# Second-layer attention of a two-block transformer kernel: rounds in two parts, the last q, k unit ahead of the third v unit, low parts as steps of their own

## The reference, cut to what matters

```python
s1 = jnp.einsum('bhqd,bhkd->bhqk', qb1, k1).astype(jnp.float32) * scale
s2 = jnp.einsum('bhqd,bhkd->bhqk', qb2, k2).astype(jnp.float32) * scale
p1 = jax.nn.softmax(jnp.where(mask, s1, -jnp.inf), axis=-1)
p2 = jax.nn.softmax(jnp.where(mask, s2, -jnp.inf), axis=-1)
a = (p1 - lam * p2).astype(v.dtype)
return jnp.einsum('bhqk,bhkd->bhqd', a, v)
...
o = o * lax.rsqrt(jnp.mean(jnp.square(o), axis=-1, keepdims=True) + RMS_EPS)
o = (o * subln_g.astype(jnp.float32) * (1.0 - lambda_init)).astype(x.dtype)
return _merge_blocks(o) @ w_out
```

## Time and profile before

| | before |
|---|---|
| median of 3 runs | 2318.71 us (2317.28 to 2320.51) |
| the profiled execution's own time | 2320.3 us |
| its span | 2318.5 us |
| mean granted TensorE clock | 0.964 |
| PE, DVE, ACT, POOL busy | 94%, 50%, 43%, 41% of the span |
| the stage that the change touches | about 699 to 966 us |

### The profile page before, as it was taken

How to read it: one execution, slowest core, us unless ns; L and a number is a source line. 1 busy time by engine, 2 the same in 40 slices (tenths; PEclk the granted TensorE clock), 3 DMA queues, 4 the chain that set the end, 5 groups by cost and what they waited for, 6 DMA issues and landing times.

```text
span 2318.5 us, 27955 instructions
## 1 busy us (share of the span) xinstructions
PE 2186.9 (94%) x10720; PEld 1817.2 (78%) x10720; DVE 1154.2 (50%) x1852; ACT 1002.3 (43%) x2027; POOL 941.9 (41%) x714
## 2 busy tenths in 40 slices
PE   7999899999998898799999999899999999999997
PEld 6788778888877777678888878677677887888886
DVE  3545565554343666465554354666664335444322
ACT  5656444443225555244443245655543234333222
POOL 3655553343356663353343442222412343322232
PEclk9999999999999999899999997999999999999998
DMA  4111123223222221122222211111112231222221
GB/s 159 55 55 58 53 91 109 91 91 102 100 71 81 92 74 46 37 73 101 100 91 102 100 62 66 37 37 37 37 46 91 100 109 55 109 91 93 100 100 53
DMA packets 29844, 183.06 MB, mean 79 GB/s; under 512 B 3984, under 2 KB 4112, under 8 KB 11920
## 3 DMA queue, kind: packets, MB, share of 16 engines
q1 hardware_dynamic: 29712, 181.27, 22.7%
HBM read 174.97 MB, written 2.10 MB: 76 GB/s over the span
## 4 chain that ended last, share of the span: by engine, by line
PE 83%; DVE 6%; ACT 5%; issue 3%; POOL 2%; DMA 0%; SPq 0%; POOLq 0%; DVEq 0%; ACTq 0%
PE PS L1454 81%; PE PS L1579 1%; POOL LO L2743 1%; DVE bQS L2194 1%; PE PS L1692 1%; ACT HI L1778 0%; DVE aQS L2194 0%; ACT cEM L2153 0%; DVE T_f L2266 0%; DVE XL L2271 0%; DVE YH L2296 0%; PE PS L1627 0%; POOL bTQ L2801 0%; ACT bP L1994 0%; DVE LO L2194 0%
## 5 line engine op out<-in xcount | busy, mean ns | idle before, releaser
L2743 POOL TENSOR_TENSOR LO<-RAW,HI 128x512 fp32r<-128x512 f32 (+2 forms) x382 | 541.3, 1433 | 627.0 <-ACT HI L1778 626.9
L1454 PE MATMUL PS<-XH,HI 128*128 128x512 f32 (+1 forms) x1584 | 638.0, 403 | 23.9 <-DVE XL L2194 7.0
L1454 PE MATMUL PS<-XH,LO 128*128 128x512 f32 (+1 forms) x1584 | 625.2, 395 | 0.0
L1454 PE MATMUL PS<-XL,HI 128*128 128x512 f32 (+1 forms) x1584 | 619.2, 395 | 2.2 <-DVE XL L2271 2.1
L1778 ACT ACTIVATE HI<-RAW 128x512 fp32r<-128x512 f32 (+3 forms) x668 | 366.2, 608 | 171.3 <-PE PS L1454 168.0
L2194 DVE TENSOR_TENSOR LO<-RAW,HI 128x512 fp32r<-128x512 f32 (+2 forms) x286 | 305.2, 1071 | 247.2 <-ACT HI L1778 246.8
L1454 PEld LDWEIGHTS PS<-XH,HI 128*128 128x128 f32 (+1 forms) x1584 | 302.3, 191 | 86.8 <-issue 21.5
L1454 PEld LDWEIGHTS PS<-XH,LO 128*128 128x128 f32 (+1 forms) x1584 | 301.4, 190 | 66.0 <-issue 1.1
L1454 PEld LDWEIGHTS PS<-XL,HI 128*128 128x128 f32 (+1 forms) x1584 | 301.6, 191 | 64.4 <-DVE XL L2271 3.6
L1454 PE MATMUL PS<-HH,HI 128*128 128x512 f32 x528 | 205.4, 389 | 0.0
L1454 PE MATMUL PS<-HL,HI 128*128 128x512 f32 x528 | 205.4, 389 | 0.0
(11 more groups left out here) (404 smaller groups left out, 3326.6 us busy)
## 6 DMA issues: line engine op xcount, KB each, us to landing
RAW<-wall SPq DMA_DIRECT2D x138, 1024.0 KB, 4.8
RAW<-wall SPq DMA_DIRECT2D x24, 896.0 KB, 4.5
bROT<-bTQ SPq DMA_DIRECT2D x64, 64.0 KB, 2.0
RAW<-wall SPq DMA_DIRECT2D x5, 512.0 KB, 3.2
XF<-xT SPq DMA_DIRECT2D x4, 512.0 KB, 5.5
outT<-XR SPq DMA_DIRECT2D x8, 256.0 KB, 2.0
FP<-cfp SPq DMA_DIRECT2D x1, 1024.0 KB, 6.7
MKF<-cmask SPq DMA_DIRECT2D x1, 704.0 KB, 11.0
```

What stands on the lines that cost most here:

```text
L1454: return e.matmul(out, a, b, start=start, stop=stop)
L2743: return e.tensor_tensor(out, x, h.bitcast(F32), ALU.subtract)
```

## The change

1. A round is two parts with a `yield` between them (`parted`). The first part holds `dva` of item n-8, `dft` n-4, `dmix` n-2, `dfd` n-4, `dsc` n and `dfl` n-3; the second `dmx` n, `dex` n and `drc` n-1. `RATES[1]` and `RATES[6]` are doubled, so a round takes as many ticks as before.
2. The maxima leave `dsc` and are a step `dmx`; the low part of the transposed weights leaves `dft` and is `dfd`, after `dmix`.
3. Unit `bqk 7` comes ahead of `bv 2`. While `bv 2` and `bv 3` run, the rate is 1.5 and 3 times that of the other units.
4. `dno` falls into four steps, `dno` (PE), `dnt` (DVE), `doh` (ACT) and `dol` (DVE), which `scaled()` puts down so that other steps stand between those of one head.
5. `lam` and `dzero` stand behind unit `bv 0`.

No arithmetic changes. The list of steps is the same as before up to the end of the first layer and from unit `bo 1` on.

```diff
-LAGD = (4, 0, 1, 2, 3, 5, 10)
-RATES = (0.37, 0.18, 1.12, 1.4, 1.0, 0.9, 0.9)
+RATES = (0.37, 0.36, 1.12, 1.4, 1.0, 0.9, 1.8)
...
+def parted(items, parts):
+
+    for n in range(len(items) + max(lag for part in parts for _, lag in part)):
+        for part in parts:
+            for stage, lag in part:
+                if 0 <= n - lag < len(items):
+                    yield from stage(items[n - lag])
+            yield
...
     out += [("bqk", 0), ("bv", 0), ("bqk", 1), ("bqk", 2), ("bv", 1), ("bqk", 3), ("bqk", 4), ("bqk", 5), ("bqk", 6),
-            ("bv", 2), ("bqk", 7), ("bv", 3)]
+            ("bqk", 7), ("bv", 2), ("bv", 3)]
...
+        def maxima(it):
+            put("dmx", *it)
+            yield from ()
...
         def taken(it):
+            put("dft", *it)
+            yield from ()
+
+        def rest(it):
             b = ag.bank_of[("dfl",) + it]
-            freed[b] = ("ptl", put("dft", *it))
+            freed[b] = ("ptl", put("dfd", *it))
             held.remove(b)
             yield from ()
+
+        made, split = [], [0]
+
+        def scaled():
+
+            x = split[0]
+            if ("doh", x) in steps:
+                ready["bO", x] = ("ol", put("dol", x))
+                split[0] = x + 1
+            for y in range(x, x + 2):
+                if ("dnt", y) in steps and ("doh", y) not in steps:
+                    put("doh", y)
+            if made:
+                y, b = made.pop(0)
+                freed[b] = ("dtt", put("dnt", y))
+                held.remove(b)
...
                 s, b = put("dno", x, h0, h + 1), flip_bank()
                 at_bank(s, b)
-                freed[b] = ("dtt", s)
-                ready["bO", x] = ("ol", s)
+                held.add(b)
+                made.append((x, b))
+                yield
+                scaled()
+            while made or split[0] <= h:
+                scaled()
+                yield
...
-        put("lam")
-        put("dzero")
         lin["banks"] = [0, 1]
         lin["n"] = 0
         qkunit(0)
         vunit(0)
+        put("lam")
+        put("dzero")
         qkunit(1)
-        alongside(rounds([(h, i) for h in range(8) for i in range(4)], [flip, scores, power, shares, mix, taken, values], LAGD), RATES[1])
-        for kind, i in [("q", 2), ("v", 1), ("q", 3), ("q", 4), ("q", 5), ("q", 6), ("v", 2), ("q", 7), ("v", 3)]:
+        alongside(parted([(h, i) for h in range(8) for i in range(4)],
+                         [[(values, 8), (taken, 4), (mix, 2), (rest, 4), (scores, 0), (flip, 3)],
+                          [(maxima, 0), (power, 0), (shares, 1)]]), RATES[1])
+        for kind, i in [("q", 2), ("v", 1), ("q", 3), ("q", 4), ("q", 5), ("q", 6), ("q", 7), ("v", 2), ("v", 3)]:
             if kind == "q":
                 qkunit(i)
             else:
                 if i >= 2:
+                    beside[1] = (1.5, 3.0)[i - 2] * RATES[1]
                     until(lambda: done[0] >= 2 * i - 2)
                 vunit(i)
...
             elif kind == "dex":
                 h, i = a
                 n, kl = 4 * h + i, 128 * (i + 1)
-                e.wait_ge(*when("mx", "dsc", h, i))
+                e.wait_ge(*when("mx", "dmx", h, i))
```

More of the change, by code:

```diff
@@ L189 @@
     "dck": (("kh", 1), ("kl", 1)),
-    "dsc": (("qk", 1), ("mx", 1)),
+    "dsc": (("qk", 1),),
+    "dmx": (("mx", 1),),
     "dex": (("exp", 2),),
@@ L194 @@
     "dfl": (("flip", 1),),
-    "dft": (("pth", 1), ("ptl", 1)),
+    "dft": (("pth", 1),),
+    "dfd": (("ptl", 1),),
     "dob": (("dob", 1), ("dsq", 1)),
@@ L198 @@
     "dsq": (("dsa", 1), ("dsr", 1)),
-    "dno": (("dbc", 1), ("dtt", 1), ("oh", 1), ("ol", 1)),
+    "dno": (("dbc", 1),),
+    "dnt": (("dtt", 1),),
+    "doh": (("oh", 1),),
+    "dol": (("ol", 1),),
     "half": (("half", 1),),
@@ L1631, in tensor @@
                 if kb == 0:
-                    e.wait_ge(*when("ptl", "dft", h, 3))
+                    e.wait_ge(*when("ptl", "dfd", h, 3))
                     if h % 2 == 0:
@@ L2012, in scalar @@
                 act(ms, ms, ACT.Sqrt, bias=EPS5, scale=1.0 / 128).then_inc(SEM["dsa"], 1)
-            elif kind == "dno":
-                h, h0, h1 = a
-                e.wait_ge(*when("dtt", *step))
+            elif kind == "doh":
+                h, = a
+                e.wait_ge(*when("dtt", "dnt", h))
                 act(blk(bOH, h), blk(bOT, h), ACT.Copy).then_inc(SEM["oh"], 1)
@@ L2473, in vector @@
                 m.then_inc(SEM["kl"], 1)
-            elif kind == "dsc":
+            elif kind == "dmx":
                 h, i = a
                 n, kl = 4 * h + i, 128 * (i + 1)
-                c = 2 * n
+                c, step = 2 * n, ("dsc", h, i)
                 e.wait_ge(*when("qk", *step))
@@ L2499, in vector @@
                                        op1=ALU.subtract).then_inc(SEM["dmix"], 1)
-            elif kind == "dft":
+            elif kind == "dfd":
                 h, i = a
@@ L2503, in vector @@
                 h_, l_ = (bPX[:, z + p:z + p + 384 * (i + 1)].rearrange("p (k n) -> p k n", n=384)[:, :, 0:128] for z in (0, 3328))
-                e.wait_ge(*when("pth", *step))
+                e.wait_ge(*when("pth", "dft", h, i))
                 diff(l_, PS[ag.bank_of["dfl", h, i]][:, 0:128 * (i + 1)].rearrange("p (k n) -> p k n", n=128), h_).then_inc(SEM["ptl"], 1)
@@ L2514, in vector @@
                 e.reciprocal(ms, ms).then_inc(SEM["dsr"], 1)
[L2515 to L2519, removed]
+            elif kind == "dnt":
+                h, = a
+                o, made = blk(bOT, h), whole["dno", h]
+                e.wait_ge(*when("dbc", *made))
+                e.scalar_tensor_tensor(out=o, in0=o, scalar=LAMT[:, 8:9], in1=PS[ag.bank_of[made]][:, :], op0=ALU.mult,
                                        op1=ALU.mult).then_inc(SEM["dtt"], 1)
-                e.wait_ge(*when("oh", *step))
-                diff(blk(bOL, h), o, blk(bOH, h)).then_inc(SEM["ol"], 1)
+            elif kind == "dol":
+                h, = a
+                e.wait_ge(*when("oh", "doh", h))
+                diff(blk(bOL, h), blk(bOT, h), blk(bOH, h)).then_inc(SEM["ol"], 1)
             elif kind == "half":
```

## The result

The changed kernel takes 2324.57 us (median of 8 runs, 2322.2 to 2329.76) where the one before took 2318.57 us beside it. The ratio is 1.0025, 95% interval 1.0014 to 1.0037: slower by 0.25%, some 6 us. I had forecast 2292 us, with a range of 2275 to 2308 us. The profiled execution has a span of 2323.1 us and a mean clock of 0.963.

A forecast was written before the change was run, and what follows sets the result against it. PE, busy 94%, was taken as the bound, with 67 us of idle and lowered clock winnable; 4.1 + 15.6 + 2 + 5 + 0 = 26.7 us off gave a median of 2292 us, range 2275 to 2308.

The forecast's parts named there:

- The start: Stage start: PE's first wait falls from 4.8 to about 0.7 us, second stays 4 to 5; gain 4.1 us.
- The end: Last stretch, `bo 0`: fewer steps left over and interleaved head factors cut idle and clock loss; gain 15.6 us.
- The waits for `bOL`: PE's four waits at heads 4 to 7 shrink from 8.8 to about 2.5 us, each under 1.5.
- The middle: Covered units: fewer than 8 PE waits for exponentials, none over 3 us but at `bqk 7`.
- under the units: 746 to 911 us: distance between exponentials and next scores shortens PE's waits; gain 2 + 5 us, then zero.
- the terms 2, 5 and 0: Gains of 2 us from 746 to 767, 5 us from 767 to 844, zero from 844 to 911.
- the dense `bv 3`: Eight rounds at three times the rate in `bv 3`; 9 us idle and clock expected there.
- a round closes on itself: Rival, chance 0.17: maxima-to-exponentials loop of 4.0 us a round; middle gives nothing or loses, 2304 to 2311 us.
- more than 30 us of ACT's waits for the scaled maxima: Profile sign: if ACT's waits for the scaled maxima sum to over 30 us, the closed loop is there.
- Slower: Rival, chance 0.05: same loop, DVE's scaling and mix drawn out by POOL; 2 us more a round gives 2340 us.
- DVE would be busy 85% in `bv 3`: Profile sign in `bv 3`: DVE should be busy 85% or more.
- the Trainium skill's rule: DVE instructions with two SBUF inputs and GpSimd SBUF reads exclude each other; at worst 8.4 us added in `bv 3`.

The follow-up runs named there:

- fourth experiment: The changed kernel with the transposed weights' low part ahead of the mix; ratio 1.0014 to the kernel before.
- third: The changed kernel with the maxima moved to the first part, right behind the scores; ratio 0.9940 to the kernel before, median 2309.6 us.
- fifth: The changed kernel, still in two parts, with exponentials a full round after the maxima and later steps' lags one more; ratio 0.9923 to the kernel before, 2302.9 us.
- second experiment: The changed kernel with the old one-part round, its lags and step order; start, unit order, rates and factor steps stay changed; ratio 0.9890 to the kernel before, 2297.1 us.

## Why the prediction was wrong, point by point

**The start** was right. The first wait is 0.69 us for the 0.7 forecast, the second 4.67 us for 4 to 5, and alone the edit brings 5 us for 4.1.

**The end** was right in length and gain. PE's first matmul of `bo 0` begins at 939.8 us. The k-step of head 6 begins at 968.3, that of head 7 follows it at once and ends at 972.9: 33 us for the 28 to 32 forecast and the 55 before. The waits for `bOL` are two of 1.5 us, and the loss of the last stretch fell to 10.6 us for the 10 forecast. What it is made of came out near the sum as well: `bo 0` lost 24.2 us with the start alone, 18.4 with the factors' steps and 9.0 with the order and the rates besides. But the factors' steps bring 13 us in all, since they also free `bv 3`, where I had set their gain against other losses and taken zero.

**The middle** was wrong: the terms "under the units" are the step that made the sum fail. I took 2 + 5 us of gain from 746 to 844 us and zero behind it. The stretch between the start and `bo 0` lost 58.7 us for 29.2, so the terms 2, 5 and 0 together should have been some -29. It isn't the dense `bv 3` that did it: counted over the units themselves, it lost 11.4 us for 11.7 before and 9 forecast. It is what lies ahead of it: `bv 1` and `bqk 3` to `bqk 6` lost 28.2 us for 16.3 before and 9.4 forecast, `bqk 7` lost 11.0 for 0 before and 3.5 forecast, and `bv 2`, for which I had no term, 8.3 for 1.6 before. "Now half a round, 2.8 ticks of 0.67 us, lies between them" was true of `dex` and the next `dsc`, and there the gain did come: PE's waits for exponentials are 6 and fell by 6.3 us. The longest is 4.05 us, though, at 799 us in `bqk 4`, where at most 3 were forecast. But the whole round between the maxima and `dex` was given up for it: half of it went to that place and half between the scores and the maxima. I priced that only as a rival.

**The rival** "a round closes on itself" named the mechanism and even its sign in the profile (more than 30 us of ACT's waits for the scaled maxima; they are 73.8). What I held against the rival *Slower*, DVE's 18 us of idle time ahead of the long maxima, was used up: 0.3 us are left. The rival failed in its price. I compared an average loop of 4.0 us with an average round of 5.3 us and took the rope's steps for something that falls where ACT waits anyway. In the timeline above they stand inside the loop: `dcq` ahead of the maxima on DVE, `dck` behind the exponentials on ACT, and they lengthen the chain on both engines in turn: DVE's low parts of query and key take 2.48 and 2.35 us, ACT's high parts 2.6 and 1.26. The round's own cost is half to two thirds of what *Slower* gave for 2 us a round: 25 to 31 us by the runs, for 48. Its chance of 0.05 was the error, together with the 0.17 for a loss that I held to be small. That DVE would be busy 85% in `bv 3` was wrong in the same way: it is busy 23.93 of 34 us from 906 to 940, 70%, since it waits in the loop and isn't full.

**POOL's share in it** is seen in the mix, which now stands right behind POOL's scaling in time: 1130 ns for 801. With the Trainium skill's rule that I had weighed (SBUF — State Buffer, Who interferes with whom), by which such a pair excludes each other, the trace agrees; the last section shows the rows. The fourth experiment brings the mix back to 734 ns and the time hardly moves, so the mix's added length was no term of the sum. The other half of what *Slower* named went the other way: DVE's scaling got shorter, 226 ns for 432.

**What is open.** The parts of the tighter lags and of the distance aren't told apart between the third, fifth and second experiment beyond their intervals. Why the dense rates gain 7 us with the old round and nothing with the new was not tried by itself. The profiles show that with the new round the loss in `bo 0` falls from 21.8 to 10.8 us, and that in `bqk 7`, `bv 2` and `bv 3` together grows from 15.9 to 30.7. The second experiment's kernel is faster than the kernel before and the changed one, at 0.989; I made no search around it.

## What to carry to other kernels

When a round of a software pipeline is cut so that a producer and its consumer on two in-order engines stand next to each other, both engines lose the freedom to run ahead, and every other step that crosses between them is drawn into the chain. Count for each pair of steps the distance in rounds before and after, not only for the pair that the edit is meant to help: here half a round was won between exponentials and scores and a whole round lost between maxima and exponentials, and in the old round the loss of that distance alone cost some 40 us. An average busy share of two thirds says nothing against it; price such a loop where the longest side work (here the split of q and k) falls into it.

## What the runs showed of the hardware that I had not expected

The same two-element scaling on DVE took 432 ns on average in the kernel before and 226 ns in the changed one, and the mix 801 and 1130 ns. The groups of the changed kernel, 740 to 945 us:

```profile
L2544 DVE SCALAR_TENSOR_TENSOR bP<-bP,bST,bP 128x128 f32<-128x128 f32 (+3 forms) x32 | 36.2, 1130 | 13.1 <-POOL bP L2857 13.0
...
L2533 DVE TENSOR_SCALAR bST<-bST 128x2 f32<-128x2 f32 x31 | 7.0, 226 | 1.1
```

The single instructions behind the averages are of two kinds. The last row is a POOL instruction that begins just ahead of the mix in the row above it:

```profile
833.61 0.17 DVE L2533 TENSOR_SCALAR bST<-bST 128x2 f32<-128x2 f32 x1
841.82 1.75 DVE L2544 SCALAR_TENSOR_TENSOR bP<-bP,bST,bP 128x512 f32<-128x512 f32 x1 [0.91 <-POOL bP L2857]
841.75 1.27 POOL L2849 TENSOR_TENSOR bTQ<-bTQ,bROT 128x512 f32<-128x512 f32 x1
```

And two of the kernel before, with the POOL instruction that runs over the first:

```profile
851.07 0.79 DVE L2487 TENSOR_SCALAR bST<-bST 128x2 f32<-128x2 f32 x1
850.52 1.31 POOL L2796 TENSOR_TENSOR bROT<-bROT,FP 128x512 f32<-128x512 f32 x1
930.55 0.75 DVE L2498 SCALAR_TENSOR_TENSOR bP<-bP,bST,bP 128x512 f32<-128x512 f32 x1 [0.58 <-POOL bP L2809]
```

Alone, the scaling takes 0.17 us and the mix of 128x512 0.74. The scaling of 0.79 us ends at 851.86, 0.03 us behind POOL's instruction, which ends at 851.83. The mix that meets POOL's next instruction from its start takes 1.75 us, 1.0 us more than alone. In the changed kernel the mix waits for POOL's scaling, POOL goes on at once with its next instruction, and 19 of 32 mixes meet it (14 before). The scaling stands where POOL is mostly idle, since POOL waits for the reciprocals behind it: 26 of the 31 recorded ones meet no POOL instruction and take 0.17 us, for 7 of 32 before. So the length of such a DVE instruction is set by what POOL is doing when it starts as much as by its own shape.
